# Level blocks of a gated recurrent mixer made by two engines: VectorE takes one half of each in the last four chunks

## The chip, the cores and the metric

One core of a Trainium2 chip. The metric is the device time of the whole kernel in microseconds (us), from its first to its last instruction; less is better. The engines are TensorE (PE in the profile, PEld for its weight loads), VectorE (DVE), ScalarE (ACT), GpSimd (POOL) and SyncE (SP), which here issues the DMAs.

## The reference

The kernel is two blocks of a network over 2048 tokens of width 1024. The first (five mixers, one of them attention, and the projections) is not touched. The second block projects its input to 3784 columns and runs two mixers on them: a sparse attention that picks 256 keys for each query by an index score (`_dsa_mixer`), and a gated recurrence (`_hgrn2_mixer`). Then it projects both outputs back, adds the input and normalises.

The recurrence, for each of 4 heads of 128 keys and 128 values:

```python
f = lbh + (1.0 - lbh) * sigmoid(f_raw);  k = 1.0 - f;  q = silu(q)
bc = cumsum(log(f))                      # within a chunk of tokens
decay = exp(where(causal, bc[t] - bc[s], -inf))
scores[t, s] = sum_k q[t, k] * k[s, k] * decay[t, s, k]
o = scores @ v + (q * exp(bc)) @ state
state = exp(bc_last) * state + (k * exp(bc_last - bc)).T @ v
```

The decay is per key, so the scores are not a plain matmul of q and k.

## The kernel before

The second mixers (`second_mixers`) are 18 passes, k = 0 to 17. Each pass is one block of instructions for all engines (`step`), with a barrier at its end. A pass holds up to five pieces of work, called branches: the index scores of one tile of 128 tokens, the upper half of a threshold search over an earlier tile's scores (VectorE, 16 rounds), the lower half of that search (ScalarE, 16 rounds, and then VectorE makes the selection), the attention of a further tile, and one chunk of 128 tokens of the recurrence (`hgrn_chunk`, i = k, for k = 0 to 15). Tiles come in falling order, so the attended widths get smaller from pass to pass. In passes 14 and 15 there are no index scores, and in 15 no upper half of the search.

The order on each engine is written out by hand. Each branch is a generator per engine that yields a place between 0 and 1 ahead of each piece of its work, and `together` (L162) always goes on with the branch whose place is lowest. That fixes the order of the engine's instructions; nothing is reordered when it runs. For the recurrence a place is a number over N = 29.

The recurrence makes the scores of a chunk by levels. bT holds the running sums of log f, keys in partitions and the 128 tokens in columns, for 4 heads (128x512). At level l the columns fall into pairs of blocks of 2^l tokens; `halves` gives the first blocks of all pairs and the second blocks (128x256 each), `joint` the sum at the last token of each first block. The first half of E becomes (joint - b) and the second half (b - joint); ScalarE takes the exp of both in one instruction; the first half is multiplied by k and the second by q. Four matmuls of E with itself, one a head, give all products of the two halves, and VectorE copies those of this level into A under a mask. Seven levels and the diagonal make the whole triangle. The steps and their lines:

- GpSimd: `diffs(l)` (L3492 first half, L3493 second half), ke (L3505), `tilde(l)` (L3498 first half times k, L3499 second half times q), then ke and qe (L3514, L3515) and, at the end, y (L3520, L3522, L3525). Its order is diffs 0, ke, diffs 1, tilde 0, diffs 2, tilde 1 and so on. E is double (l % 2), and `diffs(l)` from level 2 on waits for the matmuls of level l-2.
- ScalarE: bT (L3461), the exps of the levels (L3465), of ke and qe (L3469, L3471), ktok (L3475), y (L3478). Between them stand its 16 rounds of the search (L3121, L3123, L3125), the attention's exps (L3268) and copies (L3283), and the index scores' relus (L3009).
- TensorE: the own-pairs matmul (L3587), the matmuls of a level (L3600), the turn of ke (L3607), the outputs (L3613, L3614), the state's update (L3619); for the attention L3360 (logits), L3366 (turns), L3373 (weighing), L3354.
- VectorE: the diagonal (L3554), `pick(l)` (L3548), which waits for the matmuls of level l and for which those of level l+2 wait, and the state (L3564). Around them stand the search (L3081, L3083, L3085), the sums of the index scores (L2988, L2992), the attention's logits (L3298) and maxima (L3303, L3305), and the selection: compare (L3157), scan (L3160), two more (L3163, L3167).

ScalarE's exp of head h waits for the negated maximum (L3305), and the output matmuls wait for pick 6:

```python
pe.wait_ge(s.picked, LEVELS)
...
pe.matmul(big[:, 6, ...], qe[:, h], state[:, h], start=True, stop=False)
```

Of the kernel before, what the change touches and what calls it, by code (L numbers as in the profile page):

```python
# [17 lines left out]
ALU = mybir.AluOpType  # L18
# [5 lines left out]
TILES = SEQ // P  # L24
# [32 lines left out]
LEVELS = 7  # L57
# [2634 lines left out]
def project_out(nc, c, mix, w_out, x_old, x_out, name, ln=None, ahead=(), held=None):  # L2692
# [12 lines left out]
    with ExitStack() as ctx:  # L2705
# [13 lines left out]
        with step(nc, "w_in0 w_in1 w_in2 w_hi w_lo par_in ahead_in m_in0 m_in1 x_in0 x_in1 x_in2 turned kept kept_lo "  # L2719
# [129 lines left out]
            def _(dve):  # L2849
# [15 lines left out]
                for u in range(TILES):  # L2865
# [30 lines left out]
INDEX_SIGNALS = "iq_ahead iq_scaled iq_turned iq_kept dots relus summed "  # L2896
ATTEND_SIGNALS = ("q_ahead g_in silus q_turned q_kept ql_ps ql_kept biased logits added maxed exps turned kept weighed "
                  "o_kept o_ps y_done ")
HGRN_SIGNALS = ("hx_in hf_ahead sigs h_tanhs h_silus f_done logf turned_hq hq_kept turned_hk hk_kept sums b_kept pairs own_set "
                "diffs h_exps tilde picked e_in e_out ee_done ke_t ktok_done ho_ps up_ps sqd rs hy_done ")  # L2900


# [507 lines left out]
def hgrn_chunk(c, b, s, proj, i):  # L3410
# [5 lines left out]
    lb, g, state, x, k, qT, kT, bT, E, A = b.lb, b.g, b.state, b.x, b.k, b.hqT, b.kT, b.bT, b.E, b.A  # L3416
# [5 lines left out]

    N = 29.0

    def halves(ap, l):

        v = ap.rearrange("p h (n a b) -> p h n a b", a=2, b=1 << l)
        return v[:, :, :, 0], v[:, :, :, 1]

    def joint(l):  # L3430
        half = 1 << l
        v = bT[:].rearrange("p h (n a b) -> p h n a b", a=2, b=half)[:, :, :, 0, half - 1]
        return spread(v, 3, half)
# [10 lines left out]
    def scalar(act):  # L3444
        yield 0.0
        act.activation(f, f, ACT.Tanh, scale=0.5).then_inc(s.sigs, 1)
        yield 2.2 / N
        act.wait_ge(s.hx_in, 32)
        act.activation(flat(qe), x[:, 0], ACT.Tanh, scale=0.5)
        act.activation(flat(ke), x[:, 2], ACT.Tanh, scale=0.5).then_inc(s.h_tanhs, 1)  # L3450
        yield 3 / N
        act.wait_ge(s.f_done, 1)
        act.preload_act_table_set(LN_EXP)
        act.activation(f, f, ACT.Ln).then_inc(s.logf, 1)
        act.wait_ge(s.turned_hq, 1)
        act.activation(qT[:], four(6), ACT.Copy, scale=0.5).then_inc(s.hq_kept, 1)
        act.wait_ge(s.turned_hk, 1)
        act.activation(kT[:], four(7), ACT.Copy).then_inc(s.hk_kept, 1)
        yield 4 / N
        act.wait_ge(s.sums, 1)  # L3460
        act.activation(bT[:], four(6), ACT.Copy).then_inc(s.b_kept, 1)  # L3461
        for l in range(LEVELS):
            yield (6.5 + 2 * l) / N
            act.wait_ge(s.diffs, 2 * (l + 1))
            act.activation(E[:, l % 2], E[:, l % 2], ACT.Exp).then_inc(s.h_exps, 1)  # L3465
            if l == 0:
                yield 7.2 / N
                act.wait_ge(s.e_in, 1)
                act.activation(ke[:], ke[:], ACT.Exp)  # L3469
                act.drain()  # L3470
                act.activation(qe[:], bT[:], ACT.Exp)  # L3471
                act.activation(dec[:], bT[:, :, P - 1], ACT.Exp).then_inc(s.e_out, 1)
        yield 23.5 / N
        act.wait_ge(s.ke_t, 1)
        act.activation(ktok, four(7), ACT.Copy).then_inc(s.ktok_done, 1)  # L3475
        yield 24.5 / N
        act.wait_ge(s.ho_ps, 1)
        act.activation(y, four(6), ACT.Copy)  # L3478
        act.drain()
        for h in range(H):  # L3480
            act.activation(E[:, 0, h], y[:, h], ACT.Square, accum_out=ss[:, h:h + 1])
        act.drain().then_inc(s.sqd, 1)
        rstd(act, c, ss[:], BD).then_inc(s.rs, 1)

    def gpsimd(pool):

        def diffs(l):
            if l >= 2:

                pool.wait_ge(s.pairs, l)  # L3490
            (e0, e1), (b0, b1) = halves(E[:, l % 2], l), halves(bT[:], l)
            pool.tensor_tensor(e0, joint(l), b0, ALU.subtract).then_inc(s.diffs, 1)  # L3492
            pool.tensor_tensor(e1, b1, joint(l), ALU.subtract).then_inc(s.diffs, 1)  # L3493

        def tilde(l):
            e0, e1 = halves(E[:, l % 2], l)
            pool.wait_ge(s.h_exps, l + 1)
            pool.tensor_tensor(e0, e0, halves(kT[:], l)[0], ALU.mult).then_inc(s.tilde, 1)  # L3498
            pool.tensor_tensor(e1, e1, halves(qT[:], l)[1], ALU.mult).then_inc(s.tilde, 1)  # L3499

        yield 6 / N
        pool.wait_ge(s.b_kept, 1)
# [24 lines left out]
    def vector(dve):  # L3527
# [17 lines left out]
        def pick(l):  # L3545
# [2 lines left out]
            dve.copy_predicated(A[:], spread(c.all[:, LEVEL[l]].bitcast(U32), 1, H), four(6 + l % 2))\  # L3548
               .then_inc(s.picked, 1)

        yield 6 / N

        dve.wait_ge(s.pairs, 1)
        dve.tensor_tensor(A[:], four(7), spread(c.ident, 1, H), ALU.mult).then_inc(s.own_set, 1)  # L3554
        for l in range(LEVELS):
            if l:
                yield (9.3 + 2 * l) / N
                pick(l - 1)
        yield 22.9 / N
        pick(LEVELS - 1)  # L3560
# [6 lines left out]
    def tensor(pe):  # L3567
# [20 lines left out]
        m.then_inc(s.pairs, 1)  # L3588
        for l in range(LEVELS):
            yield (8.4 + 2 * l) / N  # L3590
            pe.wait_ge(s.tilde, 2 * (l + 1))

            if l == 0:
                pe.wait_ge(s.b_kept, 1)
            elif l == 1:
                pe.wait_ge(s.own_set, 1)
            else:
                pe.wait_ge(s.picked, l - 1)
            for h in range(H):
                m = pe.matmul(big[:, 6 + l % 2, h * P:(h + 1) * P], E[:, l % 2, h], E[:, l % 2, h],  # L3600
                              start=True, stop=True)
            m.then_inc(s.pairs, 1)
# [318 lines left out]
```

## Time and profile before

| | us |
|---|---|
| median of three runs | 5092.66 |
| lowest and highest | 5086.92, 5093.12 |
| the profiled execution | 5090.92 |
| its span | 5089.3 |
| busy in it: TensorE | 4306.3 |
| VectorE | 2629.2 |
| ScalarE | 1917.1 |
| GpSimd | 735.2 |

The profile is of one execution. Its span runs from the first to the last instruction; the execution's own time is 1.6 us longer. The passes of chunks 12 to 15 lie at about 4571 to 4842 us of it. In a row of a timeline the first number is the start and the second the duration, and a number in brackets is how long the engine had been idle, with what ended that. "x4" is a count of merged instructions.

### The profile page before, as it was taken

The numbers are of one execution on the slowest core, as the hardware profiler recorded it, in microseconds if no ns is written. First come the engines' busy times: TensorE is split into PE (matmuls) and PEld (weight loads), VectorE is DVE, ScalarE is ACT, GpSimd is POOL, SyncE is SP. The second block draws the span as 40 slices with busy tenths as digits, with TensorE's granted clock in tenths as the row PEclk, the third lists the DMA queues.
The fourth block names the chain that finished last, engine by engine and source line by source line (L and its number), as shares of the span: only waits on it lengthen the run. The fifth ranks groups of instructions, "written<-read, shape, count | busy, mean of one in ns | idle before, by whom it ended". The sixth has DMA issues, their size and how long they took to land. (4 is left out here: it accounts for less than half of the span.)

```text
span 5089.3 us, 65555 instructions
## 1 busy us (share of the span) xinstructions
PE 4306.3 (85%) x23426; PEld 3180.4 (62%) x23426; DVE 2629.2 (52%) x5393; ACT 1917.1 (38%) x3900; POOL 735.2 (14%) x755
## 2 busy tenths in 40 slices
PE   7996999985479899999979999977788887877679
PEld 6885777774366666666657888843344544554467
DVE  3113444445555555444422111148888888887546
ACT  3112323224332333333311010123677766767621
POOL 3102111000010000000000000022223333344400
PEclk9998999986568888787889999976578888777789
DMA  5326656664356555544453121121000001000033
GB/s 186 120 108 226 222 197 227 204 208 156 108 179 209 193 194 171 166 158 154 139 183 120 67 81 66 54 61 36 19 19 19 19 19 38 19 26 30 32 132 116
DMA packets 297766, 595.85 MB, mean 117 GB/s; under 512 B 47848, under 2 KB 80268, under 8 KB 297276
## 3 DMA queue, kind: packets, MB, share of 16 engines
q1 hardware_dynamic: 297440, 591.65, 34.3%
q8 instruction: 187, 3.06, 0.2%
q14 instruction: 139, 1.14, 0.1%
HBM read 457.25 MB, written 134.27 MB: 116 GB/s over the span
## 5 line engine op out<-in xcount | busy, mean ns | idle before, releaser
L3025 PE MATMUL ds_big<-ds_ikT,ds_iqT 64*128 64x512 f32 (+3 forms) x608 | 386.1, 766 | 75.7 <-ACT ds_iqT L3002 56.0
L3492 POOL TENSOR_TENSOR ds_E<-ds_bT 128x256 f32<-128x256 f32 x112 | 73.1, 652 | 2377.3 <-ACT ds_bT L3461 2194.9
L301 PE MATMUL g_acc<-g_ws_hi,g_hT_hi 128*128 128x512 f32 (+1 forms) x1024 | 386.1, 377 | 0.0
L303 PE MATMUL g_acc<-g_ws_hi,g_hT_lo 128*128 128x512 f32 (+1 forms) x1024 | 384.5, 375 | 0.0
L302 PE MATMUL g_acc<-g_ws_lo,g_hT_hi 128*128 128x512 f32 (+1 forms) x1024 | 384.4, 375 | 0.0
L529 PE MATMUL mm_big<-mm_gw_hi,mm_ghT_hi 128*128 128x512 f32 (+1 forms) x768 | 321.9, 419 | 30.9 <-PEq L134 30.9
L3081 DVE TENSOR_SCALAR_CACHE_REDUCE ds_seen<-ds_eq,ds_num 128x2048 uint16<-128x2048 uint16 (+13 forms) x224 | 331.2, 1479 | 25.7 <-issue 3.5
L531 PE MATMUL mm_big<-mm_gw_hi,mm_ghT_lo 128*128 128x512 f32 (+1 forms) x768 | 302.4, 394 | 0.0
L530 PE MATMUL mm_big<-mm_gw_lo,mm_ghT_hi 128*128 128x512 f32 (+1 forms) x768 | 301.9, 393 | 0.0
L3121 ACT ACTIVATE ds_signs<-ds_lo,ds_at 128x2048 bf16<-128x2048 uint16 (+13 forms) x224 | 291.4, 1301 | 1.5
L328 DVE COPY g_stage<-g_acc 128x512 f32<-128x512 f32 (+1 forms) x64 | 41.5, 648 | 459.3 <-PE g_acc L303 459.3
L2988 DVE SCALAR_TENSOR_TENSOR ds_score<-ds_rel,ds_iw,ds_score 128x512 f32<-128x512 f32 (+3 forms) x266 | 217.4, 821 | 62.6 <-ACT ds_rel L3009 46.5
L3025 PEld LDWEIGHTS ds_big<-ds_ikT,ds_iqT 64*128 64x128 f32 x608 | 108.0, 234 | 210.9 <-issue 80.8
L1578 ACT ACTIVATE fox_pT<-fox_big 128x512 f32<-128x512 f32 (+3 forms) x160 | 85.3, 533 | 394.4 <-PE fox_big L1646 394.4
L347 ACT ACTIVATE g_stage<-g_acc 128x512 f32<-128x512 f32 (+1 forms) x64 | 36.2, 566 | 502.4 <-PE g_acc L303 502.4
L3009 ACT ACTIVATE ds_rel<-ds_big 128x512 f32<-128x512 f32 (+3 forms) x304 | 162.5, 538 | 163.3 <-PE ds_big L3025 88.3
L3600 PEld LDWEIGHTS ds_big<-ds_E 128*128 128x128 f32 x896 | 138.7, 235 | 135.0 <-POOL ds_E L3499 68.9
L303 PEld LDWEIGHTS g_acc<-g_ws_hi,g_hT_lo 128*128 128x128 f32 x1024 | 193.2, 189 | 35.2
L302 PEld LDWEIGHTS g_acc<-g_ws_lo,g_hT_hi 128*128 128x128 f32 x1024 | 193.4, 189 | 34.7
L301 PEld LDWEIGHTS g_acc<-g_ws_hi,g_hT_hi 128*128 128x128 f32 x1024 | 193.5, 189 | 34.5
L3373 PE MATMUL ds_big<-ds_pT,ds_ct 128*128 128x128 f32 x1088 | 169.0, 300 | 51.3 <-ACT ds_pT L3283 50.9
L3600 PE MATMUL ds_big<-ds_E 128*128 128x128 f32 x896 | 159.3, 333 | 58.5 <-POOL ds_E L3499 39.0
(542 smaller groups left out, 10167.7 us busy)
## 6 DMA issues: line engine op xcount, KB each, us to landing
fox_ow<-halves SPq DMA_DIRECT2D x600, 256.0 KB, 3.2
mm_ghT_hi<-turned SPq DMA_DIRECT2D x96, 512.0 KB, 4.2
mm_ghT_lo<-turned SPq DMA_DIRECT2D x96, 512.0 KB, 5.3
proj<-g_stage SPq DMA_DIRECT2D x112, 256.0 KB, 2.0
proj<-mm_gstage SPq DMA_DIRECT2D x80, 256.0 KB, 5.0
mm_x<-proj SPq DMA_DIRECT2D x64, 256.0 KB, 3.8
second_raw<-in_w_in SPq DMA_DIRECT2D x56, 256.0 KB, 4.0
proj<-fp_stage SPq DMA_DIRECT2D x48, 256.0 KB, 2.0
```

The lines of the kernel that those rows point to most:

```text
L301: pe.matmul(sums, hT.hi[:, k, tile], wt.hi[:, k, 0:width], start=(k == 0), stop=False)
L302: pe.matmul(sums, hT.hi[:, k, tile], wt.lo[:, k, 0:width], start=False, stop=False)
L303: mm = pe.matmul(sums, hT.lo[:, k, tile], wt.hi[:, k, 0:width], start=False, stop=(k == KD - 1))
L529: pe.matmul(sums, b.hT.hi[:, u % 3, k], wt.hi[:, k, 0:width], start=(k == 0), stop=False)
L530: pe.matmul(sums, b.hT.hi[:, u % 3, k], wt.lo[:, k, 0:width], start=False, stop=False)
L531: m = pe.matmul(sums, b.hT.lo[:, u % 3, k], wt.hi[:, k, 0:width], start=False, stop=(k == KD - 1))
L2988: d = dve.scalar_tensor_tensor(out=score[:, x:x + wd], in0=rel[:, n % 2, 0:wd], scalar=sg, in1=score[:, x:x + wd], op0=ALU.mult, op1=ALU.add)
L3025: pe.matmul(big[:, n % 2, 0:wd], iqT[o, h // 2], b.ikT[o, x:x + wd], start=True, stop=True)\
L3081: dve.tensor_scalar(seen, hi, cand, 0.0, ALU.is_ge, ALU.add, accum_out=count)
L3121: act.activation(signs, lo, ACT.Sign, bias=now, accum_out=sums[:, bit:bit + 1])
L3373: m = pe.matmul(big[:, 5, h * P:(h + 1) * P], b.ct[:, x // P + t], pT[:, (h * NP + p) % 2, t], start=(p == 0 and t == 0), stop=(x + (t + 1 ...
L3600: m = pe.matmul(big[:, 6 + l % 2, h * P:(h + 1) * P], E[:, l % 2, h], E[:, l % 2, h], start=True, stop=True)
```

## The change

In the chunks i >= TILES - 4, that is 12, 13, 14 and 15, GpSimd makes only the first half of each level's differences and products. VectorE makes the second half and signals it with signals of its own, `diffs_b` and `tilde_b`. ScalarE's exp of a level and TensorE's matmuls of a level wait for both. VectorE's new instructions stand at GpSimd's places: difference 0 ahead of the diagonal, then for each level the difference of the next level and the product of this one. Picks 0 to 5 move up by 0.4 of a place. Chunks 0 to 11 are as before.

```diff
 def hgrn_chunk(c, b, s, proj, i):
+    shared = i >= TILES - 4
+    EACH = 1 if shared else 2
...
     def scalar(act):
...
-            act.wait_ge(s.diffs, 2 * (l + 1))
+            act.wait_ge(s.diffs, EACH * (l + 1))
+            if shared:
+                act.wait_ge(s.diffs_b, l + 1)
             act.activation(E[:, l % 2], E[:, l % 2], ACT.Exp).then_inc(s.h_exps, 1)
...
     def gpsimd(pool):
...
             pool.tensor_tensor(e0, joint(l), b0, ALU.subtract).then_inc(s.diffs, 1)
-            pool.tensor_tensor(e1, b1, joint(l), ALU.subtract).then_inc(s.diffs, 1)
+            if not shared:
+                pool.tensor_tensor(e1, b1, joint(l), ALU.subtract).then_inc(s.diffs, 1)
...
             pool.tensor_tensor(e0, e0, halves(kT[:], l)[0], ALU.mult).then_inc(s.tilde, 1)
-            pool.tensor_tensor(e1, e1, halves(qT[:], l)[1], ALU.mult).then_inc(s.tilde, 1)
+            if not shared:
+                pool.tensor_tensor(e1, e1, halves(qT[:], l)[1], ALU.mult).then_inc(s.tilde, 1)
...
     def vector(dve):
...
+        def diffs(l):
+            if l >= 2:
+                dve.wait_ge(s.pairs, l)
+            e1, b1 = halves(E[:, l % 2], l)[1], halves(bT[:], l)[1]
+            dve.tensor_tensor(e1, b1, joint(l), ALU.subtract).then_inc(s.diffs_b, 1)
+
+        def tilde(l):
+            e1 = halves(E[:, l % 2], l)[1]
+            dve.wait_ge(s.h_exps, l + 1)
+            dve.tensor_tensor(e1, e1, halves(qT[:], l)[1], ALU.mult).then_inc(s.tilde_b, 1)
+
         yield 6 / N
+        if shared:
+            dve.wait_ge(s.b_kept, 1)
+            diffs(0)
         dve.wait_ge(s.pairs, 1)
         dve.tensor_tensor(A[:], four(7), spread(c.ident, 1, H), ALU.mult).then_inc(s.own_set, 1)
         for l in range(LEVELS):
+            if shared:
+                if l + 1 < LEVELS:
+                    yield (7 + 2 * l) / N
+                    diffs(l + 1)
+                yield (7.5 + 2 * l) / N
+                tilde(l)
             if l:
-                yield (9.3 + 2 * l) / N
+                yield (9.3 + 2 * l if not shared else 8.9 + 2 * l) / N
                 pick(l - 1)
...
     def tensor(pe):
...
-            pe.wait_ge(s.tilde, 2 * (l + 1))
+            pe.wait_ge(s.tilde, EACH * (l + 1))
+            if shared:
+                pe.wait_ge(s.tilde_b, l + 1)
```

## Rows read from the trace of the kernel before

**Rows 1.** The page's first line.
```profile
span 5089.3 us, 65555 instructions
```

**Rows 2.** Busy us (instructions) by stretch, passes 12 to 15; clock, DMA share, GB/s.
```profile
4571.00:4647.00 76.00, 55.72 (x261) 37.01 (x259) 60.60 (x149) 55.07 (x125) 33.94 (x40) 0.79 0.09 32
4647.00:4717.00 70.00, 49.92 (x237) 34.90 (x237) 55.00 (x147) 51.07 (x124) 31.07 (x38) 0.76 0.09 31
4717.00:4780.00 63.00, 38.17 (x206) 30.80 (x205) 43.71 (x134) 45.01 (x115) 31.58 (x39) 0.75 0.10 34
4780.00:4842.00 62.00, 35.72 (x188) 28.08 (x186) 22.02 (x52) 42.20 (x111) 30.66 (x38) 0.73 0.09 30
```

**Rows 3.** Timeline of ScalarE, pass 13: start, us, instruction, idle before it.
```profile
4652.68 0.60 ACT L3258 ACTIVATE ds_ql<-ds_big 128x512 f32<-128x512 f32 x1 [2.17 <-PE ds_big L3331]
...
4682.44 0.63 ACT L3465 ACTIVATE ds_E<-ds_E 128x512 f32<-128x512 f32 x1 [0.34 <-issue]
...
4701.50 0.38 ACT L3283 ACTIVATE ds_pT<-ds_big 128x256 f32<-128x256 f32 x1 [1.65 <-PE ds_big L3366]
```

**Rows 4.** Timeline of GpSimd, pass 13: second half of differences 3, products 2.
```profile
4682.89 0.67 POOL L3493 TENSOR_TENSOR ds_E<-ds_bT 128x256 f32<-128x256 f32 x1
4683.52 0.73 POOL L3498 TENSOR_TENSOR ds_E<-ds_E,ds_kT 128x256 f32<-128x256 f32 x1
4684.20 0.72 POOL L3499 TENSOR_TENSOR ds_E<-ds_E,ds_hqT 128x256 f32<-128x256 f32 x1
```

**Rows 5.** Timeline of VectorE, pass 13: diagonal, logits, maximum of head 1, picks 4 and 6, scan.
```profile
4669.62 0.69 DVE L3554 TENSOR_TENSOR ds_A<-ds_big,consts_sb 128x512 f32<-128x512 f32 x1 [1.79 <-PE ds_big L3587]
...
4683.98 0.69 DVE L3298 CUSTOM_DVE_ANT_0 ds_L<-ds_big,ds_L 128x512 f32<-128x512 f32 x1 [1.01 <-PE ds_big L3360]
...
4685.01 0.15 DVE L3305 TENSOR_SCALAR ds_top<-ds_top 128x1 f32<-128x1 f32 x1
...
4700.99 0.73 DVE L3548 COPY_PREDICATED ds_A<-consts_sb,ds_big 128x512 f32<-128x512 uint32 x1
...
4706.62 1.54 DVE L3160 TENSOR_TENSOR_SCAN ds_sel<-ds_eq,ds_num,ds_at 128x640 f32<-128x640 f32 x1
4708.30 0.72 DVE L3548 COPY_PREDICATED ds_A<-consts_sb,ds_big 128x512 f32<-128x512 uint32 x1
```

**Rows 6.** Timeline of TensorE, pass 13: the first output matmuls.
```profile
4709.08 0.49 PE L3613 MATMUL ds_big<-ds_state,ds_qe 128*128 128x128 f32 x2 [0.82 <-DVE ds_A L3548]
```

**Rows 7.** Timeline of VectorE, pass 13: two-input instructions alone, and beside GpSimd.
```profile
4648.13 0.29 DVE L2997 TENSOR_TENSOR ds_score<-ds_score,consts_sb 128x128 f32<-128x128 f32 x1
...
4656.01 0.69 DVE L3532 TENSOR_TENSOR ds_f<-ds_f,ds_lb 128x512 f32<-128x512 f32 x1
...
4713.26 1.76 DVE L3313 SCALAR_TENSOR_TENSOR ds_gate<-ds_gate,ds_den 128x512 f32<-128x512 f32 x1
```

**Rows 8.** Timeline of GpSimd at the same time.
```profile
4713.21 1.26 POOL L3520 TENSOR_TENSOR ds_y<-ds_y,ds_hg 128x512 f32<-128x512 f32 x1 [9.03 <-ACTq L3482]
```

**Rows 9.** Timeline of ScalarE, pass 13: the exp of head 1.
```profile
4688.10 0.93 ACT L3268 ACTIVATE ds_L<-ds_L,ds_top 128x768 f32<-128x768 f32 x1
```

**Rows 10.** Timeline of VectorE, pass 12: diagonal, logits of head 1.
```profile
4595.72 0.69 DVE L3554 TENSOR_TENSOR ds_A<-ds_big,consts_sb 128x512 f32<-128x512 f32 x1 [1.44 <-PE ds_big L3587]
...
4611.29 0.69 DVE L3298 CUSTOM_DVE_ANT_0 ds_L<-ds_big,ds_L 128x512 f32<-128x512 f32 x1 [0.53 <-PE ds_big L3360]
```

**Rows 11.** Timeline of VectorE, pass 14: diagonal, logits of head 1.
```profile
4737.14 0.69 DVE L3554 TENSOR_TENSOR ds_A<-ds_big,consts_sb 128x512 f32<-128x512 f32 x1 [2.87 <-PE ds_big L3587]
...
4750.90 0.69 DVE L3298 CUSTOM_DVE_ANT_0 ds_L<-ds_big,ds_L 128x512 f32<-128x512 f32 x1 [2.77 <-PE ds_big L3360]
```

**Rows 12.** Timeline, pass 15: ScalarE's exps of levels 4 and 6, VectorE's scan.
```profile
4819.98 0.63 ACT L3465 ACTIVATE ds_E<-ds_E 128x512 f32<-128x512 f32 x1
...
4825.70 0.63 ACT L3465 ACTIVATE ds_E<-ds_E 128x512 f32<-128x512 f32 x1 [0.56 <-POOL ds_E L3493]
...
4829.80 2.02 DVE L3160 TENSOR_TENSOR_SCAN ds_sel<-ds_eq,ds_num,ds_at 128x384 f32<-128x384 f32 x1
```

More of the change, by code:

```diff
@@ L2898 @@
                   "o_kept o_ps y_done ")
-HGRN_SIGNALS = ("hx_in hf_ahead sigs h_tanhs h_silus f_done logf turned_hq hq_kept turned_hk hk_kept sums b_kept pairs own_set "
+HGRN_SIGNALS = ("diffs_b tilde_b hx_in hf_ahead sigs h_tanhs h_silus f_done logf turned_hq hq_kept turned_hk hk_kept sums b_kept pairs own_set "
                 "diffs h_exps tilde picked e_in e_out ee_done ke_t ktok_done ho_ps up_ps sqd rs hy_done ")
```

## The prediction

> **What bounds the kernel now.** The page gives the span, 5089.3 us; the profiled execution took 5090.92 us and the median of the runs is 5092.66 us, 1.7 us above it [rows 1]. Each pass of the second mixers is a block of its own with a barrier at its end, so a microsecond saved or lost inside a pass goes through to the end. I first cut out the passes of chunks 12 to 15 with the table of busy times by stretch: about 76, 70, 63 and 62 us [rows 2]. No engine is full in them: ScalarE has 72, 73, 71 and 68%, VectorE 80, 79, 69 and 36%, GpSimd never over 51%. Shares do not tell what ends last, so I read the idle times of each engine in order.
>
> ScalarE first. In chunk 13 it starts its run of work at 4652.7 with the copy of ql. After that its timeline names an idle time of 0.34 us at 4682.4, and none more until 4701.5 [rows 3]. It has 16 rounds of the threshold search, the attention's exps and all seven exps of the levels, and is never short of work. That matters for this change: an exp of a level starts when ScalarE gets to it, not when GpSimd has made the block.
>
> GpSimd next. Its part of a level is a chain with TensorE: the two halves of the differences (0.67 us the second), after the exp the two products (0.73 and 0.72), then TensorE's eight matmuls, then the differences two levels on [rows 4]. This chain is long, and it is what the change shortens. But it runs beside a ScalarE that is full.
>
> VectorE last. In chunk 13 it is busy from 4669.62 to the pick of level 6 at 4708.30 but for 1.01 us at 4683.98 and some gaps of about 0.2 [rows 5]. That pick is what TensorE waits for before the output matmuls [rows 6], and behind those stand the last head's turn, its weighing and the end of the pass. So the tail of a pass hangs on VectorE's order: pick 4, the selection's compare, the last maximum, the scan, pick 6.
>
> **The change, part by part.** (1) Per chunk GpSimd loses seven differences and seven products of half a block, 7 x 0.67 + 7 x 0.72 = 9.7 us. (2) VectorE gets the 14 instructions, in its order by place: difference l+1 and product l before pick l-1. (3) ScalarE's exp and TensorE's matmul each wait for a second signal. (4) Pick l-1 moves up by 0.4 of a place. The two new names in the list of signals cost nothing, they take semaphores of a set that is cleared as one range in any case. No DMA is issued or moved, so neither DMA queue has a term.
>
> Price of one VectorE instruction. The trace has none of 128x256 with both inputs in SBUF. A tensor_tensor of 128x128 takes 0.29 us and one of 128x512 takes 0.69 [rows 7]; the middle by columns is 0.42, an estimate from the two. The low end is 0.29. The high end comes from a pair beside GpSimd: the scalar_tensor_tensor of 128x512 took 1.76 us where a GpSimd product started 0.05 us before it, against 0.69 for that size alone [rows 7, 8]. It ended about as late as if it had first waited out the 1.26 us of GpSimd. By that, a half issued together with GpSimd's half costs up to 0.42 + 0.72 = 1.14. I take 0.42 in the sum: in chunks 12 and 13 VectorE runs late, and gets to its half when GpSimd has often finished its own; in 14 and 15 the blocked ones lie where VectorE would wait for ScalarE anyway.
>
> Chunk 13, walked in VectorE's order. Difference 0 falls in the 1.79 us that VectorE waits for the own-pairs matmul at 4669.62 [rows 5] and is free. The other 13 stand in the full stretch: 13 x 0.42 = 5.5. Of these the wait of 1.01 us before the logits at 4683.98 takes up 1.0, since the logits are then there. Early in the pass, before VectorE has fallen behind, products 0 and 1 meet their exp or GpSimd's half; at up to 0.7 each [rows 4], less what small gaps take in, I give them 0.5 together. 5.5 - 1.0 + 0.5 is +5.0 at the scan and at pick 6. ScalarE notices it only late: the first negated maximum is ready at 4685.16 and the exp of head 1 that needs it starts at 4688.10, 2.9 us of slack [rows 5, 9]. So the chain through ScalarE is not slower for the first half of the pass, and what GpSimd wins is not seen either, since ScalarE's exps stay where they are. In the tail, product 5 and product 6 stand behind VectorE's selection work and are later than now. **+5 us.**
>
> Chunk 12 has the same order with wider search instructions; VectorE's idle times there are 1.44 us before own-pairs, which hide difference 0, and 0.53 before the logits [rows 10]. 5.5 - 0.5 = **+5 us**.
>
> Chunk 14: idle 2.87 us before own-pairs and 2.77 before the logits of head 1 [rows 11]. The second takes in 2.8 of the 5.5, and 0.7 goes into small gaps further on: **+2 us**.
>
> Chunk 15: VectorE is idle for 40 of 62 us [rows 2], so the work itself fits. But its order is fixed. Exp 4 ends at 4820.61 [rows 12]; behind it VectorE has product 4, the logits of head 2, pick 3, difference 6 and pick 4, 0.42 + 0.69 + 0.73 + 0.42 + 0.73 = 3.0 by [rows 5, 7], and difference 6 waits for matmul 4, some 2 us more. So the selection starts near 4825.7, about 2 us after the search has ended; its small instructions were done long before the logits of head 3 and take in half of that, so 1 reaches the scan, now at 4829.80 [rows 12]. Against it stands the only exp that waited for GpSimd, 0.56 us at 4825.70 [rows 12], a gain of under 0.3. **+1 us.**
>
> Sum: 5 + 5 + 2 + 1 = +13 us. From the median, 5092.66 + 13 = 5105.7, and I say 5105. Two terms stay out of the sum: GpSimd's shorter work unblocks a few VectorE instructions, and halves issued at the same moment block each other; by the rows above either is a few us.
>
> **The rivals.** A change under 0.2%, 10 us, can't be told from none by a measurement of this kernel.
>
> *The halves run beside each other and the level chain sets the pass* (ends faster). Its place is the chain GpSimd to TensorE and back; its price is what leaves it, differences 2 to 6 and products 0 to 6: 5 x 0.67 + 7 x 0.72 = 8.4 us a chunk, 34 in four, 5059 us. For it: GpSimd waits for TensorE at nearly each level, and TensorE for GpSimd. Against it: ScalarE without a gap until 4701.5, and VectorE's order behind it. It decides once ScalarE's exps wait for GpSimd in most levels; now one in 28 does by 0.56 us. I give it 0.07.
>
> *Only the end of the chain gets shorter.* After the last exp, GpSimd still has to do two products and the two of ke and qe; 2 x 0.72 = 1.4 us a chunk, 5.8 in four: 5087 us, which is within 0.2%. For it, ScalarE is idle by then; against it, TensorE waited for pick 6, not for GpSimd. 0.10.
>
> *VectorE takes the new work into slack I count as used.* The 2.9 us before ScalarE notices would have to hold at the tail as well, and the search's end would have to be the true bound. Then 0 to +5 us, about 5095. 0.23.
>
> *The port.* Each half on VectorE waits out a half on GpSimd: 13 more waits of 0.7, 9 us in each of chunks 12 to 14, and 2 in chunk 15. Then 13 + 29 = +42 at the most, and with half of the instructions blocked +27, 5120 us. The rows for it are the 1.76 against the 0.69 [rows 7, 8]. Against it: VectorE comes late, when GpSimd is idle. 0.12.
> The Trainium skill has this as a rule (SBUF — State Buffer, "SBUF: two separate sides"): VectorE instructions with two SBUF inputs and GpSimd instructions that read SBUF share a port pair that one of them holds for its whole length. By that rule no pair of halves is made in parallel; it speaks against the change. The trace agrees in the one pair above. The skill's Perfetto Trace Analysis ("Optimizing Scalar/DVE Operations") adds that moving work between these two engines might not help.
>
> *That the change does nothing* is excluded: `shared` is true for chunks 12 to 15, and each of them runs.
>
> **How the numbers follow.** The forecast, VectorE's order as the bound, has 0.48; its own range is +7 to +22. Faster by over 0.2%: the first rival, 0.07, and a corner of the tail gain, 0.01: 0.08. Within 0.2% (5082.5 to 5102.8): the rest of the tail gain 0.09, the slack rival 0.23, and the low sixth of the forecast 0.08: 0.40. Slower: forecast 0.40 and port 0.12: 0.52. The range goes from 5086, which takes in the tail gain, to 5124, which takes in the port with half of the halves blocked; left out are the first rival and the port's far end.
>
> **What would show it.** Right: ScalarE still without gaps to its last level exp; in chunk 13 the scan and pick 6 about 5 us later after own-pairs than 38.7 us, and VectorE busy without its 1.01 us gap. GpSimd's busy time in the four passes falls by about 39 us, VectorE's rises by 24 to 40; a median near 0.42 for VectorE's halves, with some over 0.8 where GpSimd is at work. TensorE's wait for GpSimd's product turns in part into one for VectorE's. The port would show as medians near 1.1. I would be wrong on the mechanism if the passes of 12 and 13 were shorter than 76 and 70 us, or if ScalarE had waited for GpSimd's differences all along and did so no more.

## The result and the profile after

Thirteen runs of the changed kernel have a median of 5110.56 us (5094.57 to 5120.58), thirteen of the kernel before 5086.92 us (5071.15 to 5097.88). The ratio is 1.004, with a 95% interval of 1.0025 to 1.0055: **the change makes the kernel slower, by about 20 us** (12.7 to 28). The forecast was 5105 us, from a median of three runs of before that lay 6 us above that of all thirteen; the forecast of the shift was +13.

| one profiled execution each, us | before | after |
|---|---|---|
| span | 5089.3 | 5109.4 |
| busy: VectorE | 2629.2 | 2651.9 |
| busy: GpSimd | 735.2 | 701.5 |
| busy: ScalarE | 1917.1 | 1918.6 |
| the four passes, gate to gate | 267.7 | 287.6 |

"Gate to gate" is a cut that can be made alike in every kernel here: from VectorE's multiply by the gate at the end of one pass (L3318) to that of the next. The busy times by stretch of the changed kernel with these cuts, passes 12 to 15 (columns: stretch, its length, then TensorE, weight loads, VectorE, ScalarE, GpSimd, the granted clock, DMA share, GB/s):

```profile
4573.14:4654.61 81.47, 58.67 (x248) 39.09 (x248) 63.08 (x161) 54.81 (x124) 22.71 (x24) 0.74 0.09 30
4654.61:4729.77 75.16, 52.50 (x236) 36.76 (x236) 58.63 (x161) 51.29 (x124) 22.97 (x24) 0.74 0.08 29
4729.77:4798.32 68.55, 40.43 (x204) 32.62 (x204) 48.68 (x148) 45.23 (x115) 22.75 (x24) 0.73 0.09 31
4798.32:4860.69 62.37, 37.34 (x184) 29.22 (x184) 28.74 (x66) 42.10 (x111) 23.85 (x24) 0.70 0.09 30
```

and of the kernel before, with the same cuts instead of the round ones of [rows 2]:

```profile
4573.35:4647.34 73.99, 54.40 (x248) 35.77 (x248) 60.16 (x147) 54.48 (x124) 32.23 (x38) 0.78 0.09 33
4647.34:4717.40 70.06, 49.98 (x236) 35.06 (x236) 55.00 (x147) 51.07 (x124) 31.40 (x38) 0.77 0.09 31
4717.40:4780.68 63.28, 38.45 (x204) 30.98 (x204) 43.71 (x134) 45.01 (x115) 31.25 (x38) 0.75 0.10 34
4780.68:4841.05 60.37, 35.08 (x184) 27.73 (x184) 21.33 (x51) 42.20 (x111) 30.66 (x38) 0.73 0.09 31
```

The passes are 7.5, 5.1, 5.3 and 2.0 us longer, 19.9 in all, which is the whole of the difference of the spans. ScalarE does the same work (193.4 against 192.8 us). TensorE does the same 872 matmuls and is busy for 189 instead of 178 us: part of that is its clock, which comes up again below.

**Where in the pass.** I cut each pass at VectorE's diagonal, the scan and pick 6. From the diagonal to the scan the passes 12 to 15 took 40.02, 37.00, 32.38 and 28.70 us before and 44.92, 41.54, 36.11 and 29.43 after: +4.9, +4.5, +3.7, +0.7, together +13.9 (138.1 to 152.0). The start of the pass, gate to diagonal, grew by 2.7 in all, the end, pick 6 to gate, by 4.2, and the piece from the scan to pick 6 became 1.0 shorter. That makes 6.0 us outside the stretch from the diagonal to the scan.

**Who waits for whom.** The groups of ScalarE's instructions in the four passes (line, operation, count, then busy us, mean ns, then idle time before them in us, with its releasers), before:

```profile
L3465 ACT ACTIVATE ds_E<-ds_E 128x512 f32<-128x512 f32 x28 | 17.4, 623 | 1.6 <-POOL ds_E L3493 0.6 <-issue 0.3
L3268 ACT ACTIVATE ds_L<-ds_L,ds_top 128x896 f32<-128x896 f32 (+3 forms) x16 | 14.0, 878 | 3.9 <-DVE ds_top L3305 3.7
L3283 ACT ACTIVATE ds_pT<-ds_big 128x512 f32<-128x512 f32 (+3 forms) x28 | 13.9, 498 | 15.4 <-PE ds_big L3366 14.7
```

and after:

```profile
L3470 ACT ACTIVATE ds_E<-ds_E 128x512 f32<-128x512 f32 x28 | 17.4, 622 | 1.6 <-issue 0.2
L3268 ACT ACTIVATE ds_L<-ds_L,ds_top 128x896 f32<-128x896 f32 (+3 forms) x16 | 14.1, 879 | 11.0 <-DVE ds_top L3305 10.6
L3283 ACT ACTIVATE ds_pT<-ds_big 128x512 f32<-128x512 f32 (+3 forms) x28 | 13.9, 498 | 24.3 <-PE ds_big L3366 23.7
```

The exps of the levels wait as little as before (1.6 us): here the change had nothing to gain. The attention's exps wait 6.9 us more for VectorE's maximum, and the copies of the turned probabilities 9.0 more for TensorE. TensorE's level matmuls show a part of why the second is late (same columns), before and after:

```profile
L3600 PE MATMUL ds_big<-ds_E 128*128 128x128 f32 x224 | 38.3, 325 | 24.7 <-POOL ds_E L3499 24.7
```
```profile
L3630 PE MATMUL ds_big<-ds_E 128*128 128x128 f32 x224 | 41.1, 341 | 33.5 <-POOL ds_E L3504 17.7 <-issue 8.3 <-DVE ds_E L3568 7.4
```

The wait for GpSimd fell by 7 us, and 7.4 us of wait for VectorE's products came in its place, with 8.3 under "issue". The profile names one releaser for a wait for several signals, so I also compared the ends of the products: VectorE's was the last of the two at 17 of the 28 levels, among them all from level 2 on in chunks 12 to 14, and GpSimd's at 11. In TensorE's order the attention's turns stand behind the level's matmuls, and wait with them.

### The profile page after: what moved, and what is told of

The parts are those of the page before. It is cut to its first block and busy times, and to the rows that moved or that the text cites. A ratio compares the mean times of both kernels' runs of the same rounds, so it can differ in the third digit from the quotient of the medians.

```text
span 5109.4 us, 65583 instructions
## 1 busy us (share of the span) xinstructions
PE 4310.7 (84%) x23426; PEld 3179.1 (62%) x23426; DVE 2651.9 (52%) x5449; ACT 1918.6 (38%) x3900; POOL 701.5 (14%) x699
## 3 DMA queue, kind: packets, MB, share of 16 engines
q14 instruction: 138, 1.13, 0.1%
```

## The experiments

The theories at the start. **Load**: VectorE's order sets the time from the diagonal to the scan, and the 14 instructions cost their own length there. **Rivals**: the waits that came with them, the port that VectorE and GpSimd share, and a gain of the shorter level chain that is hidden under a larger loss. One table collects the results; the first column of numbers is what VectorE's work changes by in the four passes, at the durations measured with nothing beside it (0.42 us a half, and 0.50 less for a narrow pick). The others are of one profile each (diagonal to scan; gate to gate; ScalarE's idle before the attention's exps for the maximum, before the copies for TensorE), and the ratio of the runs' times to the kernel before. The profiled execution is one of the runs, and it lies between 10 us below the median of its kernel (left_out) and 14 above it (pick_first). How much two profiles differ without a cause can be read from only_15, whose passes 12 to 14 have the instructions of the kernel before: they took 205.1 us, against 207.3. So a difference of 2 or 3 us between two profiles shows nothing by itself. Two kernels, give_one and only_15, are not in the table.

| kernel | VectorE's work | diagonal to scan | gate to gate | waits for maximum | waits for turns | ratio (95%) |
|---|---|---|---|---|---|---|
| narrow_before | -14.1 | 133.3 | 261.8 | none | 14.5 | 0.9998 (0.9985 to 1.0011) |
| left_out | 0 | 136.9 | 264.2 | 3.4 | 14.3 | 0.9994 (0.9982 to 1.0006) |
| before | 0 | 138.1 | 267.7 | 3.7 | 14.7 | 1 |
| waits_only | 0 | 144.1 | 270.5 | 6.5 | 18.5 | 1.0021 (1.001 to 1.0033) |
| narrow_after | +9.4 | 145.3 | 277.4 | 3.2 | 24.9 | 1.0018 (1.0005 to 1.003) |
| load_only | +23.5 | 150.7 | 279.4 | 10.9 | 18.8 | 1.0038 (1.0024 to 1.0052) |
| after | +23.5 | 152.0 | 287.6 | 10.6 | 23.7 | 1.004 (1.0025 to 1.0055) |
| pick_first | +23.5 | 156.0 | 292.1 | 17.4 | 23.0 | 1.0047 (1.0032 to 1.0063) |
| all_on_v | +47.0 | 161.0 | 298.0 | 22.5 | 23.2 | 1.0044 (1.0029 to 1.0059) |
| gpsimd_more | 0 | 164.6 | 297.6 | 0.8 | 26.3 | 1.0061 (1.0041 to 1.0081) |

### left_out: GpSimd relieved, VectorE not loaded

```diff
-                yield (7.5 + 2 * l) / N
-                tilde(l)
...
-                act.wait_ge(s.diffs_b, l + 1)
...
-                pe.wait_ge(s.tilde_b, l + 1)
...
-            act.activation(E[:, l % 2], E[:, l % 2], ACT.Exp)
+            act.activation(E[:, l % 2], E[:, l % 2], ACT.Copy if shared else ACT.Exp, scale=0.001 if shared else 1.0)
```

VectorE's difference, product and their waits are gone, the picks are back at their old places. The second halves of the blocks of chunks 12 to 15 are not made, and the exp of a level is a copy of the same size.

> In chunks 12 to 15 GpSimd makes only the first halves, as in the change, and nobody makes the second halves; the exp of a level is a scaled copy there, so that stale halves stay small. So the recurrence's scores of these four chunks are left wrong. VectorE's order is that of the kernel before. It shows what GpSimd's shorter work is worth when it costs VectorE nothing. If the full engines are ScalarE and VectorE, as I forecast: 0 to 8 us less than before, passes 12 to 15 together 0 to 8 us shorter than 267.7 us. If the level chain between GpSimd and TensorE set the passes: about 34 us less, each pass about 8 us shorter.

Measured 5084.45 us against 5084.08 before. GpSimd's work in the four passes fell from 125.5 to 89.1 us, and TensorE's idle time before the level matmuls from 24.7 to 15.8:

```profile
L3617 PE MATMUL ds_big<-ds_E 128*128 128x128 f32 x224 | 38.3, 325 | 15.8 <-POOL ds_E L3502 15.8
```

9 us of waiting went. The profile's four passes are 3.5 us shorter, but its execution is the one 10 us below the median, and the runs show no gain; their interval goes from 9 us less to 3 more. So the rival by which the level chain sets the pass (34 us) falls. A gain of a few us stays possible by the runs, and the rival of a gain at the end of the chain was priced at 5.8. Against that one stands the profile: from pick 6 to the gate the four passes take 38.0 us here, and 37.6 before.

### load_only: the load without the data

```diff
+                    extra_d(l + 1)
+                yield (7.5 + 2 * l) / N
+                extra_t(l)
```

The kernel before, with 14 tensor_tensors of 128x256 at the change's places, which read constants and write a spare tile. They wait for nothing and nobody waits for them. Picks 0 to 5 stand at the change's places too.

> The kernel before with 14 more VectorE tensor_tensor instructions of 128x256 in each of chunks 12 to 15, at the places of the change and picks at its places, but on constants and into a spare tile, so that nothing waits for them and they wait for nothing; GpSimd makes both halves as before. If VectorE's added work is the cost: 13 to 22 us more than before, as with the change. If the new waits are the cost: 0 to 5 us more. If the port were the cost: more than the change, since GpSimd has twice the instructions to meet, 25 us or over, and a median of the new instructions clearly above 0.42 us.

Measured 5106.89 us, ratio 1.0038: 12 to 26 us more than before. From the diagonal to the scan it takes 12.6 us more than before, beside the change's 13.9, and ScalarE waits for the maximum as after the change:

```profile
L3551 DVE TENSOR_TENSOR ds_spare<-consts_sb 128x256 f32<-128x256 f32 x56 | 30.3, 557 | 0.1
```
```profile
L3268 ACT ACTIVATE ds_L<-ds_L,ds_top 128x896 f32<-128x896 f32 (+3 forms) x16 | 14.1, 879 | 11.2 <-DVE ds_top L3305 10.9
```

So more work on VectorE is enough to bring about nearly all of the cost, with no data in it and no wait. Two things go with it. GpSimd makes both halves here, and 13 of the 56 new instructions took over 0.8 us: they sum to 31.2 us where the change's halves take 27.6 and undisturbed ones would take 23.5. And the picks have moved, which no kernel here does alone.

### waits_only: the waits without the load

```diff
+            if l >= 2:
+                dve.wait_ge(s.pairs, l)
...
+            dve.wait_ge(s.h_exps, l + 1)
```

The kernel before, with the change's waits in VectorE's order and no work behind them, and the picks at the change's places.

> The kernel before, with VectorE in chunks 12 to 15 waiting for bT, the matmuls and the exps at the places where the change has its differences and products, picks at the places of the change, but with no work there; GpSimd makes both halves as before. If VectorE's added work is the cost: 0 to 6 us more than before. If the new waits in VectorE's fixed order are the cost: 14 to 22 us more.

Measured 5094.9 us, ratio 1.0021. By the medians that is 10.8 us more than before (5 to 17 by the interval), which is above the 0 to 6 that I gave for the case in which the load is the cost and below the 14 to 22 for the case in which the waits are. The waits, with the moved picks, are a cost of their own that the prediction had nearly left out. In the profile, of an execution 7 us below the median, they cost 6.0 us from the diagonal to the scan. With 12.6 for the load, the two sum to 18.6, over the 13.9 of both together, so they overlap. The likely reason is that a VectorE that has more work arrives later at the same waits; the moved picks, which both kernels have, may be another part.

### pick_first: another order of the same work

```diff
+                if l:
+                    yield (6.9 + 2 * l) / N
+                    pick(l - 1)
                 if l + 1 < LEVELS:
                     yield (7 + 2 * l) / N
                     diffs(l + 1)
```

The changed kernel, with pick l-1 ahead of the difference l+1 and the product l.

> The change with each pick l-1 ahead of difference l+1 (place 6.9 + 2l in place of 8.9 + 2l) in the four chunks. Both wait for the same matmul, and TensorE's level l+1 waits for the pick. If VectorE's load is the cost, the order between the two is worth under 4 us either way against the change, so 15 to 24 us more than before. If late picks hold TensorE's levels back, it wins 5 us or more on the change.

Measured 5109.02 us, ratio 1.0047, which can't be told from the change. The profile, of the slowest of its six runs, has 4 us more from the diagonal to the scan, and 17.4 us of waits for the maximum. The order of the picks is no way out.

### all_on_v: both halves on VectorE

```diff
-    EACH = 1 if shared else 2
+    EACH = 0 if shared else 2
...
+            dve.tensor_tensor(e0, joint(l), b0, ALU.subtract)
...
+            dve.tensor_tensor(e0, e0, halves(kT[:], l)[0], ALU.mult)
```

> The change, with both halves of each level on VectorE in chunks 12 to 15 and none on GpSimd: 28 instructions a chunk in place of 14. If VectorE's load sets these passes, the other 14 cost about as much again, each 0.42 us with little to hide them: 35 to 50 us more than the kernel before, and the time from the diagonal to the scan grows by about 28 us over the four passes against before (14 with the change). If the port between the two engines were the cost, nothing is left to meet here: as before or less than the change's 20 us.

Measured 5108.05 us against 5086.66, ratio 1.0044. The dose is doubled and the time is not: 21 us instead of the 35 and more that I expected. In the passes it does show, diagonal to scan +22.9 against +13.9, and the waits for the maximum double:

```profile
L3268 ACT ACTIVATE ds_L<-ds_L,ds_top 128x896 f32<-128x896 f32 (+3 forms) x16 | 14.1, 880 | 22.8 <-DVE ds_top L3305 22.5
```

Its profile lies 10 us above its median, and it has four runs; by the two ratios with their intervals it may lie anywhere between 9 us below the change and 13 above. So the second 23.5 us of VectorE work most likely cost less than the first, which cost about 20; in the stretch from the diagonal to the scan it was 9.0 after 13.9. In this kernel GpSimd makes no part of the levels, so that no half waits for one of the other engine; that is the likely reason, and it was not tried by itself.

### gpsimd_more: the chain made longer instead of shorter

```diff
+            if shared:
+                more(l, 0)
...
+            if shared:
+                more(l, 1)
```

The kernel before, with one more GpSimd instruction of 128x256 on constants ahead of the differences and of the products of each level.

> The kernel before with 14 more GpSimd instructions of 128x256 in each of chunks 12 to 15, one ahead of each difference and each product, on constants into a spare tile. It lengthens the level chain by 14 x 0.6 = 8 us a chunk and leaves VectorE's order alone. If the chain has slack behind ScalarE and VectorE, part of it is taken in: 5 to 20 us more than before in all. If the chain sets the passes: 30 us or more. If the port matters, VectorE's two-input instructions in these passes take longer than before.

Measured 5117.16 us against 5086.66, ratio 1.0061: 30 us (21 to 41 by the interval). I had given 5 to 20 for a chain with slack and 30 or more for one that sets the passes, so this is the second case: with 42 us more, the chain does set them. Here the exps of the levels do wait for GpSimd, 18.8 us where it was 0.6:

```profile
L3468 ACT ACTIVATE ds_E<-ds_E 128x512 f32<-128x512 f32 x28 | 17.5, 627 | 19.7 <-POOL ds_E L3503 18.8 <-issue 0.4
L3268 ACT ACTIVATE ds_L<-ds_L,ds_top 128x896 f32<-128x896 f32 (+3 forms) x16 | 14.1, 878 | 1.2 <-DVE ds_top L3305 0.8
```

Together with left_out this is the shape of the thing: 36 us less for GpSimd give nothing that the runs show, 42 more cost 30. The chain was just short enough not to be seen. Not all of the 30 need be the chain's: the small steps of VectorE's search at L3085 took 16.9 us here and 11.5 before, and the same 479 VectorE instructions of the four passes sum to 201.4 us against 193.2. That was the sign named ahead for the port.

### give_one: work moved the other way

```diff
+            r = rel[:, n % 2, 0:wd]
+            pool.tensor_tensor(r, r, iw[:, 2, h:h + 1].broadcast_to([P, wd]), ALU.mult)
+            pool.drain()
+            pool.tensor_tensor(score[:, x:x + wd], score[:, x:x + wd], r, ALU.add).then_inc(s.summed_p, 1)
```

The kernel before, with the last index head's sums taken from VectorE and made by GpSimd as a product and a sum, in every pass that has more than one block of index scores.

> The other direction, on the kernel before: in the passes whose index scores have more than one piece (tiles 4 to 15), the sum of index head 7 goes from VectorE to GpSimd, as a product by the sign and an addition. 36 sums move. VectorE loses 36 x about 0.8 = 30 us of work, GpSimd gets some 90 us in its idle time. If VectorE's load sets the passes: 8 to 30 us less than before. If GpSimd's level chain is held up by it, or the port blocks VectorE for as long: no change or slower.

Measured 5108.5 us against 5086.66, ratio 1.0053: slower, where I expected 8 to 30 less. In its profile passes 12 to 15 take 265.9 us, 1.8 less than before, with 2.5 us for the maximum instead of 3.7. By the measure of only_15 that is no difference. But the edit is in the wider passes too, and there the sums are long: on GpSimd 1.10 and 1.55 us in the place of one VectorE instruction of 0.82 us, the mean of these sums in the kernel before. The relu's buffer is held all the while, which is the likely reason for the loss:

```profile
L3048 POOL TENSOR_TENSOR ds_score<-ds_score,ds_rel 128x512 f32<-128x512 f32 (+3 forms) x36 | 55.9, 1553 | 5.1
L3046 POOL TENSOR_TENSOR ds_rel<-ds_rel,ds_iw 128x512 f32<-128x512 f32 (+3 forms) x36 | 39.5, 1098 | 127.3 <-DVE ds_score L2995 114.3 <-ACT ds_rel L3020 13.0
```

The ten passes before chunk 12 sum to 1053.2 us against 1028.8. So in passes 12 to 15 the kernel says nothing against the load theory, and little for it; that work taken from VectorE would gain time in the wider passes, it did not bear out.

### only_15: the change in the last chunk alone

```diff
-    shared = i >= TILES - 4
+    shared = i >= TILES - 1
```

> The change in chunk 15 alone, where VectorE is idle for 40 of 62 us. If VectorE's load is the cost, pass 15 is within 1 us of its 60.4 us of before, apart from what its fixed order costs (I forecast +1); passes 12 to 14 are as before. If the waits in VectorE's order cost much, pass 15 is 2 us or more longer.

A single run, 5094.45 us. Pass 15 took 60.07 us gate to gate, against 60.37 before; diagonal to scan 30.1 against 28.7. Where VectorE is idle for two thirds of the pass, the halves cost about as much before the scan as I forecast (+1), within what two profiles differ by, and nothing over the whole pass. There is nothing to win there either.

### narrow_before and narrow_after: room made on VectorE

```diff
+            w = 16 if shared else P
-            dve.copy_predicated(A[:], spread(c.all[:, LEVEL[l]].bitcast(U32), 1, H), four(6 + l % 2))\
+            dve.copy_predicated(A[:, :, 0:w], spread(c.all[:, LEVEL[l]].bitcast(U32), 1, H)[:, :, 0:w], four(6 + l % 2)[:, :, 0:w])\
```

The runs so far added work. These two take some away, at the places where the halves stand: a pick of 128x64 took 0.23 us instead of 0.73. The one is the kernel before, the other the changed kernel.

> The kernel before, with VectorE's seven picks of each of the chunks 12 to 15 cut from 128x512 to 128x64, at the same places and with the same waits; of A, only the first 16 columns of each head are picked, so the scores of these chunks are not the reference's. A pick should fall from 0.73 to about 0.25 us: some 3.4 us less work for VectorE in each pass, 13 in all, after the diagonal. If VectorE's order alone sets the time from the diagonal to the scan (138.1 us in the four passes before), that falls by 2.5 to 3 in chunks 12 and 13, 1 to 2 in 14 and under 1 in 15: 7 to 9 us in all, and the time by as much. If another engine's chain (ScalarE with its rounds and exps, TensorE with the attention and the levels) is just as long, so that only more work for VectorE shows and less does not, as it was for GpSimd, it falls by 0 to 3 us.

> The changed kernel with the same narrow picks in chunks 12 to 15; the scores of these chunks are again not the reference's. VectorE then has 14 halves more (5.9 us) and 3.4 us less in a pass. If VectorE's order alone sets the stretch, the halves cost the same as with whole picks: diagonal to scan 12 to 14 us over that of the kernel before with narrow picks, and 145 to 147 us in all. If there is another chain about as long as VectorE's, the narrow picks make room for a part of the halves: 4 to 9 us over the kernel before with narrow picks, about 143 in all. If with that room GpSimd's shorter level chain were worth anything, it would be at or below the kernel before with narrow picks.

Measured 5084.93 us without the change and 5096.87 with it, against 5087.33. Without the change, 14.1 us less work gave 4.8 us before the scan, between the two expectations, and nothing that the runs show (ratio 0.9998, from 8 us less to 6 more). ScalarE's groups tell where it ends:

```profile
L3268 ACT ACTIVATE ds_L<-ds_L,ds_top 128x896 f32<-128x896 f32 (+3 forms) x16 | 14.0, 876 | 0.3
```

The 3.7 us for which ScalarE had waited for the maximum are gone, and with them, it seems, what there was to gain; what stands behind that, ScalarE's own work or another chain, was not tried. With the change and the same room, the time is still 12 us longer, and 12.0 us from the diagonal to the scan, as I had given for the case in which VectorE's order alone sets the stretch. But it comes much less through the maximum: that wait is 3.2 us, and the one for TensorE's turns is 24.9.

```profile
L3268 ACT ACTIVATE ds_L<-ds_L,ds_top 128x896 f32<-128x896 f32 (+3 forms) x16 | 14.1, 878 | 3.6 <-DVE ds_top L3305 3.2
L3283 ACT ACTIVATE ds_pT<-ds_big 128x512 f32<-128x512 f32 (+3 forms) x28 | 14.0, 499 | 25.6 <-PE ds_big L3366 24.9
```

Level 5 of chunk 12 shows what TensorE waited for:

```profile
4615.28 0.61 ACT L3470 ACTIVATE ds_E<-ds_E 128x512 f32<-128x512 f32 x1
...
4616.27 0.73 POOL L3504 TENSOR_TENSOR ds_E<-ds_E,ds_kT 128x256 f32<-128x256 f32 x1
...
4620.39 0.83 DVE L3569 TENSOR_TENSOR ds_E<-ds_E,ds_hqT 128x256 f32<-128x256 f32 x1
...
4621.32 1.13 PE L3631 MATMUL ds_big<-ds_E 128*128 128x128 f32 x8 [3.08 <-POOL ds_E L3504]
```

GpSimd's product was done 1.11 us after the exp. VectorE had the logits, a pick, the next difference, the maximum, a sum of index scores and the end of the search ahead of its own, which was done 5.32 us after the exp, and the matmuls began 0.10 us later. (The row names GpSimd, whose product of level 6 had just ended as well.) With narrow picks and without the change these matmuls began 2.43 us after the exp. At levels 5 and 6 of chunks 12 to 14 VectorE's product was the last each time, at 17 of the 28 levels in all.

So there are two ways by which the halves cost time. One is their length ahead of the maxima (load_only shows it alone: 18.8 us for the turns, 10.9 for the maximum). The other is that TensorE's level matmuls, with the attention behind them, now depend on VectorE's order (narrow_after shows it best, since its wait for the maximum is no longer than in the kernel before).

## Why the prediction was right, and by how much it was off

**The mechanism** was that VectorE's order sets the time from the diagonal to the scan, and that the halves' length is paid there. load_only bears it out with 12.6 us beside 13.9. The sum by chunk was +5, +5, +2, +1; that stretch measured +4.9, +4.5, +3.7, +0.7. The step that was off is **chunk 14**: I let its idle time of 2.77 us before the logits [rows 11] take up the halves. It went, but ScalarE then waited for the maximum of head 2, late in the pass:

```profile
4778.74 0.83 ACT L3268 ACTIVATE ds_L<-ds_L,ds_top 128x640 f32<-128x640 f32 x1 [2.02 <-DVE ds_top L3305]
```

**The waits** had next to no term in the sum: 0.5 us for products 0 and 1 in chunk 13, and the wait for matmul 4 in chunk 15. waits_only shows that they cost 6.0 us before the scan and 10.8 in the time, moved picks included. The load by itself was +5.0, +3.2, +2.8 and +1.5 by chunk in load_only, so that the sum met the stretch is in part luck: in chunk 13 the load alone gave 3.2 of my 5, and the change 4.5.

**The price of a half** was taken as 0.42, between 0.29 and 1.14. Of the 56, 47 took under 0.5 us, 6 over 0.8:

```profile
L3563 DVE TENSOR_TENSOR ds_E<-ds_bT x28: 398/422/982, 4594.3 to 4841.1; 128x256 f32<-128x256 f32 x28
...
L3568 DVE TENSOR_TENSOR ds_E<-ds_E,ds_hqT x28: 410/422/1287, 4598.9 to 4845.7; 128x256 f32<-128x256 f32 x28
```

(count: shortest/median/longest ns, first and last start.) The median was right. The sum of the 56 is 27.6 us, 4 more than at 0.42 each. The reason I gave, that VectorE comes late and finds GpSimd done, was right only in part; the last section has the rest.

**ScalarE without gaps** was wrong. I had read 2.9 us of slack at one exp, that of head 1 in pass 13 [rows 9], and let it stand for the half pass. At the last head's exp there was none to spare: the 3.7 us of waits for the maximum in the group of before are 1.29, 1.42, 0.67 and 0.28 at the exps of head 3, the last, in the four passes. In passes 12 to 14 after the change that exp waits no more, but head 2's does, 2.40, 2.09 and 2.02 us. In pass 13 this is ahead of the last level exp:

```profile
4707.95 0.94 ACT L3268 ACTIVATE ds_L<-ds_L,ds_top 128x768 f32<-128x768 f32 x1 [2.09 <-DVE ds_top L3305]
...
4709.26 0.62 ACT L3470 ACTIVATE ds_E<-ds_E 128x512 f32<-128x512 f32 x1
```

For the sum it made no difference, since I counted the delay at the scan in any case.

**What the sum lacked** is the 6 us outside that stretch. The largest single piece is at the end of pass 12. I had said that products 5 and 6 come late behind the selection. TensorE then waits, and afterwards works at half its clock. Its timeline after the change:

```profile
4627.83 0.81 PE L3360 MATMUL ds_big<-ds_cT,ds_ql 128*128 128x384 f32 x2
4632.50 2.04 PE L3630 MATMUL ds_big<-ds_E 128*128 128x128 f32 x8 [3.86 <-DVE ds_E L3568]
...
4637.12 2.07 PE L3360 MATMUL ds_big<-ds_cT,ds_ql 128*128 128x512 f32 x2
4638.98 1.92 PE L3630 MATMUL ds_big<-ds_E 128*128 128x128 f32 x8
```

and the same steps before, where product 5 was there 0.72 us after TensorE was ready:

```profile
4629.01 1.16 PE L3600 MATMUL ds_big<-ds_E 128*128 128x128 f32 x8 [0.72 <-POOL ds_E L3499]
...
4631.48 1.12 PE L3360 MATMUL ds_big<-ds_cT,ds_ql 128*128 128x512 f32 x2
4632.44 1.05 PE L3600 MATMUL ds_big<-ds_E 128*128 128x128 f32 x8
```

The stretches by busy time have the granted clock in the third column from the right, after and before:

```profile
4634.80:4641.50 6.70, 6.70 (x18) 3.85 (x17) 5.42 (x15) 1.09 (x2) 0.00 (x0) 0.50 0.00 0
```
```profile
4630.30:4634.60 4.30, 4.30 (x25) 2.82 (x23) 3.95 (x6) 1.68 (x3) 2.93 (x3) 1.00 0.00 0
```

6.70 us of matmuls at 0.50 (1.2 GHz) are 3.35 at 1.00 (2.4 GHz), so this stretch was up to 3.3 us too long, and TensorE was full in it. The output matmuls started 3.16 us after the start of pick 6 instead of 0.78, since the turn of ke and the attention's weighing were still ahead of them: before, TensorE had waited for that pick, and now it came to it late. load_only, whose pass 12 had a mean clock of 0.85 instead of 0.74, took 77.67 us for it, against 81.47 after the change and 73.99 before. When the clock falls differs from run to run, so a part of the 6 us belongs to the one profile.

**The rivals.** The level chain (0.07) falls by left_out. So does the end of the chain (0.10) as an account of the whole, since the change is slower. Whether a gain of its size, 5.8 us, is hidden in the sum, the runs can't tell; against it speaks only the profile of left_out, whose ends are not shorter. VectorE's slack (0.23), 0 to 5 us in all: excluded by load_only. The port (0.12), priced at +27 with half of the halves blocked: 6 of the 56 took over 0.8 us, and the median is 0.42. A small part of it is there, but it cost VectorE no more than before. The halves took 4 us more than at 0.42 each, and the instructions that both kernels have took 4.6 less, 188.6 us in the four passes against 193.2. The small step of the search (L3085, 48 of them) fell from 11.5 to 9.9 us and the four scans from 6.6 to 5.6, with GpSimd at work for 33 us less. VectorE's busy time rose by 18.9 us only, below the 24 to 40 that I gave: the halves are 27.6, the rest is 4.6 less, and in the profile's rows 4.1 more of the instructions' time overlaps that of the next, which busy time counts once. GpSimd's fell by 33 instead of 39, mostly because its remaining halves got longer (products 0.77 to 0.85 us, differences 0.64 to 0.72).

## What to carry to other kernels

Before work goes from one engine to another, look for who waits for the engine that loses it, and take those waits as the most that can come back: here the exps waited 0.6 us for GpSimd, and 36 us less of GpSimd work bought nothing that the runs show. Waits of an engine that has time to spare don't count: TensorE had waited 24.7 us for GpSimd, 9 of them went in left_out, and the time did not follow. An engine whose results are waited for a little (3.7 us) in an order written by hand has little room: of 23.5 us added to VectorE 12.6 came out at the scan and about 19 (12 to 26) in the kernel's time, and 14.1 taken away gave 4.8 at the scan and nothing in the time that can be told from none. Splitting an instruction over two engines also puts a second wait in front of its reader, and what stands behind the reader in its queue is late too.

## What the hardware did that I had not expected

Two halves issued together are not made together. In pass 13 the exp of level 1 released both engines at 4685.7:

```profile
4685.70 0.43 DVE L3568 TENSOR_TENSOR ds_E<-ds_E,ds_hqT 128x256 f32<-128x256 f32 x1 [0.97 <-ACT ds_E L3470]
4685.75 1.08 POOL L3504 TENSOR_TENSOR ds_E<-ds_E,ds_kT 128x256 f32<-128x256 f32 x1 [2.21 <-ACT ds_E L3470]
```

VectorE's took its 0.43 us and GpSimd's 1.08 in place of 0.73: the pair was done after 1.13 us, and 0.43 + 0.73 is 1.16. The differences at 4689.0 are alike, 0.42 and 0.85 in place of 0.61, the pair done after 0.90 us where the sum is 1.03. Where GpSimd was first, VectorE waited:

```profile
4709.95 0.72 POOL L3504 TENSOR_TENSOR ds_E<-ds_E,ds_kT 128x256 f32<-128x256 f32 x1 [3.23 <-ACT ds_E L3470]
...
4710.07 0.88 DVE L3568 TENSOR_TENSOR ds_E<-ds_E,ds_hqT 128x256 f32<-128x256 f32 x1
```

This pair took 1.00 us, where the sum is 0.42 + 0.72 = 1.14. I had bounded only this second case, from the 1.76 us of [rows 7]. In the first, where both wait for the same exp, VectorE loses nothing and GpSimd pays. GpSimd's product was then the last that TensorE waited for (11 of the 28 levels). The Trainium skill (SBUF — State Buffer, "SBUF: two separate sides") has the rule that the two engines' access of this kind excludes each other; the pairs above agree to within 0.14 us. What such a split saves is then not the time of one half beside the other, but only that VectorE's instruction is the shorter one: 1.13 us against 0.73 + 0.72 = 1.45 for the two products on GpSimd.
